# GpSimd multiplies for the modulation, VectorE sums the eight row blocks in one pass and folds each sum at once

## The reference

```
def adaln(cond, w, b):
    m = jax.nn.silu(cond) @ w + b
    return m.reshape(m.shape[:-1] + (N_MOD, D_MODEL))

def ffn_sublayer(h, m, g, w13, w2, base):
    hn = modulate(rms_norm(h, g), m[:, :, base], m[:, :, base + 1])
    return h + 0.5 * m[:, :, base + 2] * swiglu_2(hn, w13, w2)
```

## Time and profile before

| | us |
|---|---|
| median of 3 runs | 2614.36 (2614.21 to 2614.83) |
| the profiled execution's own time | 2616.11 |
| its span in the profile | 2614.3 |
| PE busy | 2465.4 (94%) |
| DVE busy | 1679.3 (64%) |
| ACT busy | 1152.9 (44%) |
| POOL busy | 1345.5 (51%) |

### The profile page before, as it was taken

How to read it: one execution, slowest core, us unless ns; L and a number is a source line. 1 busy time by engine, 2 the same in 40 slices (tenths; PEclk the granted TensorE clock), 3 DMA queues, 4 the chain that set the end, 5 groups by cost and what they waited for, 6 DMA issues and landing times.

```text
span 2614.3 us, 31053 instructions
## 1 busy us (share of the span) xinstructions
PE 2465.4 (94%) x11415; PEld 2010.5 (77%) x11415; DVE 1679.3 (64%) x1912; ACT 1152.9 (44%) x1342; POOL 1345.5 (51%) x691
## 2 busy tenths in 40 slices
PE   7998899999899889999999989889999999997998
PEld 6886667788788766778877878777778878876886
DVE  5777547677666654767767767564667566555544
ACT  4444453534444445354444444344353454444443
POOL 4994120599899212149979979930088078000000
PEclk9999999999999999999999999999999999998999
DMA  7665323666566532377767768745177577552653
GB/s 252 221 228 156 113 93 118 213 228 222 188 224 212 165 109 92 122 250 258 257 216 250 254 207 260 234 142 180 49 229 238 180 238 242 182 170 96 198 184 108
DMA packets 312484, 495.30 MB, mean 189 GB/s; under 512 B 14478, under 2 KB 221610, under 8 KB 312266
## 3 DMA queue, kind: packets, MB, share of 16 engines
q1 hardware_dynamic: 289306, 412.54, 48.8%
q0 software_dynamic: 22800, 80.54, 9.7%
q10 hardware_dynamic: 288, 1.05, 0.1%
HBM read 493.02 MB, written 1.05 MB: 189 GB/s over the span
## 4 chain that ended last, share of the span: by engine, by line
PE 72%; POOL 13%; DVE 8%; ACT 4%; issue 2%; DMA 1%; ACTq 0%; SPq 0%; DVEq 0%; POOLq 0%; PEldq 0%
PE ps L798 68%; POOL arena L729 5%; POOL arena L719 4%; DVE wlo L470 2%; POOL arena L731 2%; PE ps L1057 1%; ACT whi L457 1%; POOL arena L704 1%; PE ps L927 1%; POOL arena L750 1%; PE ps L920 0%; ACTq L389 0%; DVE ps L1931 0%; DMA arena<-in_mod_w_dram 0%; PE ps L1028 0%
## 5 line engine op out<-in xcount | busy, mean ns | idle before, releaser
L470 DVE TENSOR_TENSOR wlo<-raw,whi 128x2048 fp32r<-128x2048 f32 (+5 forms) x405 | 1073.5, 2653 | 495.3 <-ACT whi L457 490.6
L798 PE MATMUL ps<-whi,HThi 128*128 128x512 f32 (+3 forms) x2328 | 936.9, 402 | 42.5 <-ACT arena L1336 10.5
L457 ACT ACTIVATE whi<-raw 128x2048 fp32r<-128x2048 f32 (+4 forms) x405 | 753.0, 1862 | 408.9 <-PE ps L798 401.0
L798 PE MATMUL ps<-wlo,HThi 128*128 128x512 f32 (+3 forms) x2328 | 914.5, 393 | 0.0
L798 PE MATMUL ps<-whi,HTlo 128*128 128x512 f32 (+3 forms) x2328 | 914.2, 393 | 0.0
L798 PEld LDWEIGHTS ps<-whi,HThi 128*128 128x128 f32 (+1 forms) x2328 | 443.8, 191 | 145.0 <-issue 18.6
L798 PEld LDWEIGHTS ps<-wlo,HThi 128*128 128x128 f32 (+1 forms) x2328 | 443.3, 190 | 94.1
L798 PEld LDWEIGHTS ps<-whi,HTlo 128*128 128x128 f32 (+1 forms) x2328 | 444.5, 191 | 84.2
L729 POOL TENSOR_TENSOR arena<-arena 128x1024 f32<-128x1024 f32 (+1 forms) x170 | 493.1, 2900 | 9.7
L719 POOL TENSOR_TENSOR arena<-arena,cond 128x1024 f32<-128x1024 f32 x184 | 444.4, 2421 | 34.8 <-DMA arena<-in_mod_w_dram 27.3
L798 PE MATMUL ps<-whi,AThi 128*128 128x512 f32 x824 | 323.3, 392 | 5.4 <-DVE HTlo L1712 4.2
(11 more groups left out here) (212 smaller groups left out, 1564.3 us busy)
## 6 DMA issues: line engine op xcount, KB each, us to landing
raw<-in_ffn_w_dram SPq DMA_DIRECT2D x330, 512.0 KB, 4.7
raw<-in_w_ffn_gu_dram SPq DMA_DIRECT2D x176, 512.0 KB, 4.8
arena<-in_mod_w_dram POOLq DMA_DIRECT2D x144, 512.0 KB, 4.9
raw<-in_w_ffn_down_dram SPq DMA_DIRECT2D x88, 512.0 KB, 4.3
raw<-in_w_in_dram SPq DMA_DIRECT2D x40, 1024.0 KB, 5.1
raw<-in_even_w_in_dram SPq DMA_DIRECT2D x12, 1024.0 KB, 5.1
raw<-in_conv_w_in_dram SPq DMA_DIRECT2D x12, 1024.0 KB, 5.1
raw<-in_w_out_dram SPq DMA_DIRECT2D x8, 1024.0 KB, 5.0
```

The source lines that it names most:

```text
L457: i = nc.scalar.activation(whi[0:rows, r, a:b], raw[0:rows, r, a:b], ACT.Copy)
L470: i = nc.vector.tensor_tensor(wlo[0:rows, r, a:b], raw[0:rows, r, a:b], whi[0:rows, r, a:b].bitcast(F32), ALU.subtract)
L798: return nc.tensor.matmul(o, lhsT, rhs, start=first, stop=last)
```

## The change

GpSimd now makes only the two multiplications of each sum, into one of two buffers of 128x2048 (`mod_product`, now in the arena), and waits before it writes a buffer until VectorE has summed the one that stood there (`mods_taken`). The additions on GpSimd are gone.

VectorE's new `take_sum` takes one sum: one reduction over the eight row blocks, which reads the 128x2048 products with the row block as the innermost index (so that successive elements lie 256 elements apart) and writes 128x256, then at once the transpose and the reduction of the fold. In the FFN with `n` sums, `take_sum` stands once in each of steps 1 to 8, between `wlo` of units B and C, and once more at the end of as many of the steps 0, 2, 4, 6, 7, 5 as are wanted, in this order. So FFNs 0 and 1 take two sums in steps 2, 4, 5, 6 and 7; FFNs 2 and 3 in 2, 4 and 6; FFN 4 in 2, 4, 6 and 7; FFN 5 in 2 and 4; FFNs 6 and 7 in none.

`folded` only makes the small matrix, in step 9 of the FFN. The waits of TensorE for GpSimd at the ends of FFNs are gone, as is GpSimd's wait for `mods_summed` ahead of FFNs 4 to 7. In FFN 0 a sum is now 256 wide when it is folded, and 512 before.

```
-        mod_product = [flatPJ[:, 2048:4096], flatPJ[:, NPJ:NPJ + 2048]]
+        mod_product = [arena[:, 0:2048], arena[:, 2048:4096]]
+        mod_acc = [flatPJ[:, 2560:2560 + MOD], flatPJ[:, 2560 + MOD:2560 + 2 * MOD]]
...
-                    for st, acc in enumerate(accs):
+                    for st in range(n_s):
+                        k = acc_made[0]
+                        if k > 1:
+                            pool.wait_ge(s_taken, k - 1)
                         for half in range(2):
                             if st == 0:
                                 pool.wait_ge(s_mod[half], 16 * units_before[0])
                             by = cond[:, 4 * half:4 * half + 4, st:st + 1].broadcast_to([P, 4, MOD])
-                            p = nc.gpsimd.tensor_tensor(mod_product[at][:, 1024 * half:1024 * half + 1024].rearrange("p (c n) -> p c n", c=4),
+                            p = nc.gpsimd.tensor_tensor(mod_product[k % 2][:, 1024 * half:1024 * half + 1024].rearrange("p (c n) -> p c n", c=4),
                                                         mod_raw[at][half].rearrange("p (c n) -> p c n", c=4), by, ALU.mult)
-                            if st == len(accs) - 1 and i + 1 < len(part):
+                            if half:
+                                p.then_inc(s_made, 1)
+                                pool.wait_ge(s_made, k + 1)
+                                acc_made[0] += 1
+                            else:
                                 link(p)
+                            if st == n_s - 1 and i + 1 < len(part):
                                 mod_load(part, 2 * i + 2 + half, at)
-                            elif half:
-                                link(p)
-                        q = mod_product[at]
-                        n = 4 * MOD
-                        while n > acc.shape[-1]:
-                            link(nc.gpsimd.tensor_tensor(q[:, 0:n], q[:, 0:n], q[:, n:2 * n], ALU.add))
-                            n //= 2
-                        p = nc.gpsimd.tensor_tensor(acc, q[:, 0:n], q[:, n:2 * n], ALU.add)
-                        p.then_inc(s_made, 1)
-                        pool.wait_ge(s_made, acc_made[0] + 1)
-                        acc_made[0] += 1
...
-                    if ph["f"] >= 4:
-                        pool.wait_ge(sem("mods_summed"), min(ph["f"] - 1, 5))
...
-                if ph["mods"] and not ph["hosts"]:
-                    pe.wait_ge(s_made, made_by[f])
...
+            def take_sum(f):
+
+                k = sums_taken[0]
+                a = k - (made_by[f] - sums_in[f])
+                acc = mod_acc[k % 2]
+                dve.wait_ge(s_made, k + 1)
+                V.tensor_reduce(out=acc, in_=mod_product[k % 2].rearrange("p (c n) -> p n c", c=DC), op=ALU.add, axis=AX_X).then_inc(s_taken, 1)
+                dve.wait_ge(s_taken, k + 1)
+                link(V.transpose(acc, acc))
+                V.tensor_reduce(out=fold_of(f)[:, a * (MOD // 32):(a + 1) * (MOD // 32)],
+                                in_=acc.rearrange("p (k j) -> p k j", j=32), op=ALU.add, axis=AX_X)
+                sums_taken[0] += 1
 
             def folded(share):
 
-                for f in share[0]:
-                    fold(f)
                 lanes = lanes_of(share)
...
                         split_lo(dve, u0 + 4, lead)
+                        if lead in sums_at:
+                            take_sum(f)
+                        if lead == GROUPS - 2 and f in shares:
+                            folded(shares[f])
                         split_lo(dve, u0 + 5, lead)
 
                     f = ph["f"]
+                    n_sums = sums_in[f] if f < len(mods) else 0
+                    sums_at = range(GROUPS - 2 - min(n_sums, GROUPS - 3), GROUPS - 2)
+                    also_at = (0, 2, 4, 6, 7, 5)[:n_sums - len(sums_at)]
...
-                        if f == 2 and i < 2:
-                            fold(1, len(accs_of(1)) - 2 + 2 * i)
-                        if ph["mods"] and i in fold_after[f]:
-                            fold(f, fold_after[f][i])
+                        if i in also_at:
+                            take_sum(f)
...
-                    if f == 7:
-                        folded(shares[f])
...
-                    if ph["hosts"]:
-                        folded(shares[f])
```

More of the change, by code:

```diff
@@ L231, in program @@
         flatPJ = PJ.rearrange("p b n -> p (b n)")
[L232 to L239, removed]
@@ L249, in modulation @@
[L249 to L259, removed]
@@ L260, in program @@
-        made_by = [sum(len(acc) for part in mods[:f + 1] for _, _, acc in part) for f in range(len(mods))]
+        mod_raw = [[flatPJ[:, 0:1024], flatPJ[:, 1024:2048]], [flat[:, 0:1024], flat[:, 3072:4096]]]
+        mod_product = [arena[:, 0:2048], arena[:, 2048:4096]]
+        mod_acc = [flatPJ[:, 2560:2560 + MOD], flatPJ[:, 2560 + MOD:2560 + 2 * MOD]]
+        fold_home = [flat[:, 0:MOD], flat[:, 0:MOD], flat[:, 14 * MOD:15 * MOD], flat[:, 4 * MOD:5 * MOD],
+                     flatPJ[:, MOD:2 * MOD], flatPJ[:, 0:MOD], flatPJ[:, 0:MOD], flatPJ[:, 2048:2048 + MOD]]
@@ L261, in program, with modulation @@
+        def modulation(spans):
+            return [(l, m, 2 if l == 0 and m * MOD < 5 * D else 1) for l, first, last in spans for m in range(first, last)]
+        mods = [modulation(spans) for spans in
+                ([(0, 0, 7)], [(0, 7, 14)], [(0, 14, 20)], [(0, 20, 32)], [(0, 32, 36), (1, 0, 9)], [(1, 9, 20)], [(1, 20, 28)], [(1, 28, 36)])]
+        sums_in = [sum(n_s for _, _, n_s in part) for part in mods]
+        made_by = [sum(sums_in[:f + 1]) for f in range(len(mods))]
         shares = {f: (fs, [x for g in fs for x in mods[g]])
@@ L262, in program @@
                   for f, fs in ((0, (0,)), (2, (1, 2)), (3, (3,)), (4, (4,)), (5, (5,)), (7, (6, 7)))}
-        def accs_of(f):
-            return [acc for _, _, accs in mods[f] for acc in accs]
         def fold_of(f):
-            acc = accs_of(f)[0]
-            return fold_home[f][:, 0:len(accs_of(f)) * acc.shape[-1] // 32]
+            return fold_home[f][:, 0:sums_in[f] * (MOD // 32)]
         def lanes_of(share):
@@ L369, in program @@
         s_mod = [sem(f"mod_landed{h}") for h in range(2)]
-        s_made = sem("mods_made")
+        s_made, s_taken = sem("mods_made"), sem("mods_taken")
         first_unit, u = [], 0
@@ L710, in modulate @@
                     mod_load(part, half, at)
-                for i, (_, m, accs) in enumerate(part):
+                for i, (_, m, n_s) in enumerate(part):
                     beside(i)
                     units_before[0] += 1
-                    for st, acc in enumerate(accs):
+                    for st in range(n_s):
+                        k = acc_made[0]
+                        if k > 1:
+                            pool.wait_ge(s_taken, k - 1)
                         for half in range(2):
@@ L838, in sums_of @@
                 for f in share[0]:
-                    accs = accs_of(f)
-                    n, halves = len(accs) * (MOD // 32), accs[0].shape[-1] // MOD
-                    r = fold_of(f).rearrange("p (a h k) -> p h a k", h=halves, k=MOD // 32)
-                    for h in range(halves):
-                        i = mm(ps[:, bank, at:at + n], lanes_of(share), r[:, h], h == 0, h == halves - 1)
+                    n = sums_in[f] * (MOD // 32)
+                    i = mm(ps[:, bank, at:at + n], lanes_of(share), fold_of(f))
                     at += n
@@ L1721, in merged_lo @@
                     i.then_inc(sem("merged_lo"), 1)
-            accs_folded = [0] * len(mods)
-            def fold(f, upto=None):
-                accs = accs_of(f)
-                w, done = accs[0].shape[-1], accs_folded[f]
-                upto = len(accs) if upto is None else upto
-                if upto > done:
-                    dve.wait_ge(s_made, made_by[f] - len(accs) + upto)
-                for a in range(done, upto):
-                    link(V.transpose(accs[a], accs[a]))
-                    o = fold_of(f)[:, a * w // 32:(a + 1) * w // 32]
-                    i = V.tensor_reduce(out=o, in_=accs[a].rearrange("p (k j) -> p k j", j=32), op=ALU.add, axis=AX_X)
-                    if a == 0:
-                        link(i)
-                accs_folded[f] = upto
+            sums_taken = [0]
+            def take_sum(f):
[9 more added lines that the diff above has]
+                sums_taken[0] += 1
             def folded(share):
-                for f in share[0]:
-                    fold(f)
                 lanes = lanes_of(share)
@@ L1752, in mod_add @@
                 at, owed = 0, []
-                for (l, n_s), parts in itertools.groupby(share[1], lambda x: (x[0], len(x[2]))):
+                for (l, n_s), parts in itertools.groupby(share[1], lambda x: (x[0], x[2])):
                     parts = list(parts)
@@ L1992, in _ @@
                             split.upto(last + RING)
```

(3 more changed lines are left out.)

5 lines of the change are left out of this document (removed).

## The result

The changed kernel takes 2641.86 us (median of 4 runs, 2639.01 to 2644.43), the kernel before 2614.28: a ratio of 1.0104, with a 95% interval of 1.0088 to 1.012. It is 27.6 us slower; 15 were forecast (2629 us, with a range from 2578 to 2676). The profiled execution has a span of 2640.2 us, 25.9 more than before.

The account below looks back on a forecast made before the run. TensorE, busy 2465.4 of 2614.3 us, was taken as the bound, so only its idle 149 us counted. Costs of 57 us less gains of 42 made 15 more: 2614.4 + 15 = 2629 us, range 2578 to 2676.

Parts of the forecast that it names:

- What goes, 42 us: TensorE's waits for GpSimd's late sums and for mods_folded, with the clock behind them, go: 42 us saved.
- FFN 5: Two TensorE waits for the product of gate and up go, with the clock behind them: 13 us saved.
- the end of FFN 1: TensorE's 7.3 us wait for GpSimd's last sum goes, with 1.3 of clock: 8.6 us saved.
- the end of FFN 0: Splits ahead of the residual are no longer lengthened by GpSimd: 2.8 of 3.2 us of TensorE's waits saved.
- the ends of FFNs 3, 4 and 5, where the signal stood: Three TensorE waits for mods_folded, 13.5 us, go with their clock: 17.5 us saved.
- The reduction: VectorE's new reduction over eight row blocks takes 3.5 us, at 1.64 ns for each element read with a step.
- the rival by results: Reduction runs near the adjacent pace or costs by result, 2.3 to 3.1 us: 2575 to 2597 us; chance 0.25.
- A step with one sum costs nothing: FFN steps with one sum: product of gate and up ends at 2543.9, wanted at 2546.9, so nothing lost.
- A step with two, alone: 15 two-sum FFN steps, alone or first: 1.4 us wait plus 0.9 clock, 2.3 each, 35 us in all.
- In a row: The other 7 two-sum steps, following another such step: 2.8 us each, no clock beyond it, 20 us in all.
- The norm's scaling in FFNs 3 and 5: Scaling for the hosted norm also stands in step 2 there: about 1.2 us each, 2 in all.
- Rival 3: Reduction pace as forecast, but GpSimd does not hold unit C and the clock stays: 29 us faster, 2585; chance 0.14.

Follow-up runs that it names:

- Experiment 2: Changed kernel with every reduction reading 256 elements, seven of each sum's eight row blocks left out: 2569.1 us, ratio 0.9821 to the kernel before.
- experiment 8: Changed kernel with adjacent reads, small matrix and signal mods_folded of FFNs 3, 4 and 5 put back behind the last residual additions: 2584.11 us, ratio 0.9884.
- experiment 1: Changed kernel with GpSimd writing products row block innermost, so that VectorE's reduction reads adjacent elements: 2573.81 us, ratio 0.9843 to the kernel before.
- experiment 3: Changed kernel with seven of eight row blocks left out only in sums at the ends of steps: 2574.46 us, ratio 0.9842 to the kernel before.
- experiment 4: Changed kernel with GpSimd multiplying 32 of each block's 256 columns from the third sum on: 2594.94 us, ratio 0.9919 to the kernel before.

## Why the prediction was right, point by point

In short: the direction and the mechanism were right, and the time lay inside the range, but the change was nearly twice the 15 us forecast. The costs were 16 us too low and the gains 5 us too low, so the total looks closer than its largest term was.

- *What goes, 42 us.* Experiment 2 measured 47. Read step by step, its trace against that of the kernel before gives: FFN 5 14.0 (13 forecast), the end of FFN 1 7.7 (8.6), the end of FFN 0 3.2 (2.8), and the ends of FFNs 3, 4 and 5, where the signal stood, 4.8 + 9.5 + 5.0 = 19 (17.5). The 5 us on top are two places that were priced at nothing: step 1 of FFN 4, 4.0 us, whose wait of 2.0 the prediction named and left out, and step 3 of FFN 0, 1.3 us. Of the 19, the place of the signal is some 10 (experiment 8); the rest, the folds at the borders with their clock, was not tried alone. TensorE's own waits for VectorE at the end of FFN 0 shrank by 1.9 us (3.2 to 1.3), not 2.8.
- *The reduction.* The choice of 1.64 ns for an element, from the one row that read with a step, was right in kind, and the rival by results was wrong (experiment 1). In size the step of 256 elements costs 1.81 ns. The estimate from the 1.73 ns of the Trainium skill (Vector Engine (DVE) Microarchitecture Reference, section 5.2), 3.7 us, was nearer to 3.87. The section's 2.5 ns, from which the prediction made 5.3 us, stands there for both sources or the destination alone at a small step, and not for one source; nothing here ran at it.
- *A step with one sum costs nothing.* Right: experiment 3, and in the table no single step from 1 on lost anything but step 3 of FFN 4 (0.7), behind a late one and with a held scaling of 1.73 us. FFN 3's step 0, with one sum right ahead of the product, lost 1.2, which I had not priced. Against the kernel of experiment 2, step 1 of FFN 4 (one sum, and the final norm's work) lost 2.2 too.
- *A step with two, alone.* 1.4 us of wait and 0.9 of clock were taken. The wait is 1.9 (two reductions 0.37 us longer would give 2.1 in place of 1.4), and the step loses 2.0 to 2.3 without the clock, 3.8 to 3.9 with it; over all 15 the mean is 3.3. There is a part that I did not see: about 0.4 us more than the wait is lost though the clock stays at 1.00 (2.29 for 1.9). It could have been read before: the wait of 0.9 us in the earlier trace rows had cost its step 1.3, at a clock of 1.00, and in experiment 4 waits of 20.5 us in all go with 28 us lost in double steps.
- *In a row.* Forecast 2.8 each; steps 5 to 7 of FFN 0 lost 4.6, 1.5 and 2.2, of FFN 1 1.6, 3.0 and 3.2, step 7 of FFN 4 4.5: 2.9 on the mean of the seven.
- *The norm's scaling in FFNs 3 and 5*, 1.2 us each: the two steps lost 6.0 and 6.5, where 2.3 + 1.2 were forecast. This is the largest miss of a single place. The prediction let GpSimd hold only splits; here it held the scaling too (1.73 us in place of 0.29), so that scaling with its reciprocals took 2.2 us, against 0.8 in experiment 4, and TensorE's wait of 4.2 us was followed by a clock of 0.86 and 0.72.
- *The sum.* 57 us were forecast for the costs and 73 measured (experiment 2). The reduction's 0.37 us, twice in each of 22 steps, gives 16 by itself: the term that was mis-sized is the price of an element. (The steps do not show it so cleanly. Twice 0.37 more would make 3.0 for a lone step and 3.5 for one in a row, and they lost 3.3 and 2.9: the terms beside it were off too, by up to 0.6 us a step, in both directions.) The waits themselves were 50.8 us in 25, where 50 in 22 were forecast. That this agrees is in part luck, since the prediction's own terms add up to 43 us of waits (15 x 1.4 + 7 x 2.8 + 2.4). The other 20 us of the double steps are lost behind them. With gains 5 us higher the total came to 26 by spans.
- *Rival 3* said that GpSimd's hold does less harm, and priced its absence at 44 us (15 slower turned into 29 faster). The hold is there in the steps shown, and experiment 4, which takes it away, gives back 47 us.

## What to carry to other kernels

A reduction over the outer index is a matter of layout before it is one of engines: let the engine that writes the operand put at least two of the summed elements side by side. Before work is moved onto an engine that has idle time on the mean, add up its fullest step, with the time that its operations stand held beside another engine's, and look for the operation in the step that another engine waits for; here one slow sum to a step was nearly free, and a second one in some of the steps cost 3 us each. And a wait that stands on the critical path goes by making early what it waits for; here the wait alone cost nothing.

## What the runs showed of the hardware

- A reduction of 128x2048 float32 to 128x256 takes 2.28 us where the eight summed elements are adjacent, 2.28 where they are four adjacent pairs 512 elements apart, and 3.87 where each is 256 elements from the next.
- GpSimd's multiplication of 128x1024 takes 1.90 us (its shortest: 1.89) writing adjacent elements, the same (1.89) writing every second, and 2.05 at its shortest writing every eighth.
- Reductions and 32x32 transposes of VectorE are not held by GpSimd: 3.60 to 3.95 us over 92 reductions, 0.445 to 0.448 over 92 transposes. Splits (two inputs of 128x2048) are: 2.29 us on the mean where GpSimd's instructions are short (experiment 4), and 3.28 in the step shown, begun while a multiplication was in flight. A VectorE operation with one 128x128 matrix and a scalar for each partition (`TENSOR_SCALAR`) is held too: 0.28 to 0.29 us in most places, 1.73 to the end of a multiplication in three.
- A short wait costs TensorE more than its length: waits of 0.9 and 1.9 us lost 1.3 and 2.3 us of a step at a clock of 1.00. Why was not tried.
- The same wait of 1.9 us was followed by a clock of 1.00 in FFN 0 and of 0.57 for some 4 us in FFN 3. What makes the difference was not tried.
